# Three more weight slots for the experts, taken from tiles that the mixing has finished with

## What is computed

```python
for l in range(DEPTH):                                    # DEPTH = 2
    xn = rms_norm(x, norm_mix[l])
    c_q, c_kv, k_rope, dq, dk, dv, mu, mv, mo, mg = jnp.split(xn @ w_in[l], split_at, axis=-1)
    y_mla = mla_mixer(c_q, c_kv, k_rope, ...)
    y_dil = dilated_mixer(dq, dk, dv, rel_bias, ...)      # scores + a bias that depends on the distance
    y_ml = mlstm_mixer(mu, mv, mo, mg, ...)
    x = x + jnp.concatenate([y_mla, y_dil, y_ml], axis=-1) @ w_out[l]
    x = x + hier_moe(rms_norm(x, norm_ffn[l]), ...)

def hier_moe(x, wg, bg, we, be, w_gate, w_up, w_down):
    ...                                                   # comb: two experts for each token
    h = jax.nn.silu(jnp.einsum('bsd,edf->bsef', x, w_gate)) * jnp.einsum('bsd,edf->bsef', x, w_up)
    h = h * comb[..., None].astype(h.dtype)
    return jnp.einsum('bsef,efd->bsd', h, w_down)
```

## Time and profile before

| | us |
|---|---|
| median of 3 runs | 2033.39 |
| lowest and highest of them | 2032.96, 2038.36 |
| the profiled execution | 2034.52 |
| its span, first to last instruction | 2032.8 |
| PE busy in the span | 1945.6 |
| DVE busy | 472.4 |
| ACT busy | 318.0 |
| mean granted TensorE clock, share of full speed | 0.983 |

### The profile page before, as it was taken

The page is one execution under the profiler, slowest core; times in us unless marked ns, Lnnn a source line. Parts: engine busy times, 40 slices in busy tenths (PEclk is TensorE's granted clock), DMA queues, the critical chain, the costliest instruction groups (busy, mean ns, idle before and its releaser), DMA issues.

```text
span 2032.8 us, 26560 instructions
## 1 busy us (share of the span) xinstructions
PE 1945.6 (96%) x11730; PEld 1468.8 (72%) x11730; DVE 472.4 (23%) x1233; ACT 318.0 (16%) x831; POOL 4.8 (0%) x11
## 2 busy tenths in 40 slices
PE   6999999999889999999899999999998899999998
PEld 6788888788756666556597888877877556665555
DVE  2323223222201110221133241323221121110212
ACT  2122122210211100111022221221111111100110
POOL 0000000000000000000000000000000000000000
PEclk9999999999999999999999999999998999999999
DMA  8343342224499999999953333331255999999996
GB/s 322 149 188 124 125 152 97 88 83 165 192 425 420 412 428 406 407 404 405 427 195 158 132 125 124 125 130 42 88 200 237 426 409 411 406 428 409 404 408 272
DMA packets 39302, 536.03 MB, mean 264 GB/s; under 512 B 4648, under 2 KB 4776, under 8 KB 6672
## 3 DMA queue, kind: packets, MB, share of 16 engines
q1 hardware_dynamic: 38160, 531.46, 64.2%
q0 software_dynamic: 768, 2.77, 0.4%
q10 hardware_dynamic: 256, 0.04, 0.0%
HBM read 532.13 MB, written 2.12 MB: 263 GB/s over the span
## 4 chain that ended last, share of the span: by engine, by line
PE 95%; issue 3%; DVE 1%; DMA 1%; ACT 0%; SPq 0%; DVEq 0%
PE ps L624 93%; PE ps L675 1%; DMA ring<-in_w_lat 1%; PE ps L968 0%; PE ps L691 0%; PE ps L683 0%; PE ps L889 0%; PE ps L1008 0%; ACT PR L1831 0%; SPq L550 0%; PE ps L762 0%; ACT L1844 0%; DVE v_mla L1547 0%; PE ps L802 0%; DVE PR L1589 0%
## 5 line engine op out<-in xcount | busy, mean ns | idle before, releaser
L624 PE MATMUL ps<-ring,scr 128*64 128x256 f32 (+2 forms) x5184 | 717.2, 434 | 47.7 <-issue 47.0
L624 PEld LDWEIGHTS ps<-ring,scr 128*64 128x64 f32 (+1 forms) x5184 | 413.6, 141 | 339.1 <-issue 208.0
L624 PE MATMUL ps<-ring,XN 128*128 128x256 f32 (+2 forms) x2304 | 485.8, 372 | 16.6 <-DMA ring<-in_w_lat 16.6
L624 PEld LDWEIGHTS ps<-ring,XN 128*128 128x128 f32 x2304 | 425.7, 191 | 66.3 <-issue 18.5
L624 PE MATMUL ps<-XN,ring 128*128 128x256 f32 x768 | 170.4, 381 | 0.9 <-DVE prob L1137 0.9
L624 PEld LDWEIGHTS ps<-XN,ring 128*128 128x128 f32 x768 | 144.7, 190 | 26.6 <-issue 7.7
L624 PE MATMUL ps<-PR,ring 128*128 128x256 f32 x640 | 141.3, 380 | 0.0
L624 PEld LDWEIGHTS ps<-PR,ring 128*128 128x128 f32 x640 | 120.7, 190 | 18.6 <-issue 2.7
L624 PE MATMUL ps<-v_mla,PR 128*128 128x128 f32 x1024 | 121.7, 282 | 4.0 <-DVE v_mla L1547 4.0
L624 PE MATMUL ps<-prob,PR 128*128 128x256 f32 x512 | 120.0, 389 | 4.9 <-issue 3.9
L624 PEld LDWEIGHTS ps<-v_mla,PR 128*128 128x128 f32 x1024 | 120.2, 198 | 4.1 <-issue 4.1
(11 more groups left out here) (226 smaller groups left out, 907.2 us busy)
## 6 DMA issues: line engine op xcount, KB each, us to landing
ring<-in_moe_w_gate SPq DMA_DIRECT2D x64, 2048.0 KB, 12.8
ring<-in_moe_w_up SPq DMA_DIRECT2D x64, 2048.0 KB, 13.5
ring<-in_moe_w_down SPq DMA_DIRECT2D x64, 2048.0 KB, 17.6
ring<-in_w_main SPq DMA_DIRECT2D x36, 2048.0 KB, 8.0
ring<-in_w_out_a SPq DMA_DIRECT2D x10, 2048.0 KB, 7.9
ring<-in_w_out_b SPq DMA_DIRECT2D x6, 2048.0 KB, 8.1
ring<-in_w_lat SPq DMA_DIRECT2D x4, 1472.0 KB, 16.3
ring<-in_w_up SPq DMA_DIRECT2D x2, 1664.0 KB, 16.8
```

The costliest lines, as they stand in the source:

```text
L624: return pe.matmul(o, lhsT, rhs, start=start, stop=stop, skip_group_check=True)
```

## The change

It gives the expert half nine slots. The three new ones are no new memory: slot 6 (`IN_XN`) is the tile `XN`, slot 7 (`IN_PR`) is columns 5120 to 9215 of `PR`, slot 8 (`IN_BIAS`) is the first 4096 columns of `BIAS`. The expert loads go round in the order 8, 5, 0, 1, 2, 3, 4, 6, 7. The mixing half keeps its six, begun one place earlier (`c0` in slot 5). The first load into slot 8 may go once the last bias read, `ds11`, is done, those into 6 and 7 once `ob7` is. `Y` moves from `PR` to `prob`, `Sw` from `prob` to `PR`; `combB` and `comb2` move within `PR`. The bias is overwritten, so between the layers POOL reads it back from HBM once, after the last product that reads slot 8 in layer 0 (`u1` of the last pair), and DVE waits for that in layer 1.

```diff
+IN_XN, IN_PR, IN_BIAS = NSLOT, NSLOT + 1, NSLOT + 2
+EXPERT_SLOTS = (IN_BIAS, 5, 0, 1, 2, 3, 4, IN_XN, IN_PR)
...
 def plan_slots():
 
-    r = Uses(NSLOT)
+    r = Uses(NSLOT + 3)
     r.part = "layer"
-    at, held = 0, None
+    at, held = NSLOT - 1, None
...
     for j, name in enumerate(EXPERT):
-        r.once(name, j % NSLOT)
+        r.once(name, EXPERT_SLOTS[j % len(EXPERT_SLOTS)])
...
-        Sw = probf[0:2 * CAP, 0:S]
+        Sw = prf[0:2 * CAP, at + 704:at + 704 + S]
...
-        Y = prf[0:2 * CAP, 8192:8192 + D]
+        Y = probf[0:2 * CAP, 0:D]
...
+        spare = {IN_XN: xnf, IN_PR: prf[:, at + 1024:at + 1024 + SLOT],
+                 IN_BIAS: BIAS[:, :, :].rearrange("p h n -> p (h n)")[:, 0:SLOT]}
...
         def slot(name):
-            return ring[:, SLOTS.where(name), :]
+            s = SLOTS.where(name)
+            return ring[:, s, :] if s < NSLOT else spare[s]
...
             if at > 0:
                 return ready(LAST_READER.get(before, before), l)
+            if SLOTS.where(name) == IN_BIAS:
+                return copied(f"ds{H_D - 1}", l)
+            if SLOTS.where(name) in (IN_XN, IN_PR):
+                return ready(f"ob{N_OUT - 1}", l)
             return ready(LAST_READER[before], l - 1) if l else None
...
             pool.wait_ge(bias_out, 32)
+            for l in range(DEPTH - 1):
+
+                last = [n for n in EXPERT if SLOTS.where(n) == IN_BIAS][-1]
+                pool.wait_ge(*ready(LAST_READER[last], l))
+                pool.dma_start(BIAS[:, :, :], bass.AP(bias_dram.tensor, 0, [[1, P], [2 * S, H_D], [1, S + P]])).then_inc(bias_out, 16)
+                pool.wait_ge(bias_out, 48 + 16 * l)
...
-                                dve.wait_ge(bias_out, 32)
+                                dve.wait_ge(bias_out, 32 + 16 * l)
```

More of the change, by code:

```diff
@@ L393, in build @@
         iota = prf[:, at + 640:at + 640 + CAP]
-        combB = prf[:, at:at + NE * S].rearrange("p (e s) -> p e s", e=NE)
-        Y = prf[0:2 * CAP, 8192:8192 + D]
-        comb2 = prf[:, 10240:10240 + NT * NE].rearrange("p (t e) -> p t e", t=NT)
+        combB = prf[:, at + 1024:at + 1024 + NE * S].rearrange("p (e s) -> p e s", e=NE)
+        Y = probf[0:2 * CAP, 0:D]
+        comb2 = prf[:, at + 960:at + 960 + NT * NE].rearrange("p (t e) -> p t e", t=NT)
         q_mla, k_mla = PR[:, :, MV:MV + W_M], PR[:, :, MO:MO + W_M]
@@ L454, in grow @@
             return probf[0:H_M, at:at + S]
-        slot_full = [sem(f"slot_full{s}") for s in range(NSLOT)]
+        slot_full = [sem(f"slot_full{s}") for s in range(NSLOT + 3)]
         psum_full = [sem(f"psum_full{b}") for b in range(8)]
```

## The result

The changed kernel takes 1985.14 us (median of 4 runs, 1982.98 to 1986.55), the kernel before beside it 2034.16: a ratio of 0.9755, with a 95% interval of 0.9737 to 0.9772. That is 49 us less, where 56 had been forecast (1978). The profiled execution's span is 1984.9 us, against 2032.8: 47.9 less, and this is the difference that the rest of the text accounts for.

The account below looks back on a forecast made before the run. The prediction took the DMAs to bound the expert stages, just above TensorE. Gain 58.1 us, less 1.7 (clock) and 0.3 (reload), is 56.1: 2034.5 becomes 1978.4, median about 1978; own range 1973 to 1988, 8 in 10 1967 to 1993.

Parts of the forecast that it names:

- the reload hurts: Rival: the bias reload delays layer 0's last two expert loads, with upper bounds for reload and clock; 1986 us, chance 0.12.
- What bounds the kernel: Expert stages: DMAs bind at a full queue, 58.9 us a pair against TensorE's 57.1; TensorE ready 4 us before them.
- The floor of TensorE: Rival for the expert stages: TensorE is the bound, all waits and slow clock go, 66.2 us gained; 1968, chance 0.13.
- The rate of a full queue: Expert stages: about 427 GB/s from g0 of pair 0 to the last load, no dip where dn0 is read.
- the rivals at 413 and 358 GB/s: Expert loads: 413 GB/s whatever the queue, about 2004 us, chance 0.09; 358 through the new tiles, about 2135, chance 0.02.
- The tightest place, pair 0: After g1 of pair 0 nothing is freed for 15 us; 2.9 us of queue against 2 of start just holds.
- 83 loads and 3.8 us: From g0 of pair 0 to u1 of pair 7: 83 loads of 4.91 us plus 3.8 fixed; 58.1 us gained in all.
- The stretch: From SP's first issue after g0 of pair 0 to u1 of pair 7's start; the prediction's steps give 411.4 us.
- The clock behind the last waits: Last u1 of each layer: a slow clock costs up to 1.7 us each, 0 to 3.4; 1.7 taken.
- The reload: Bias reload beside layer 0's last expert loads: delays them 2.2 us, of which 0.3 shows; bounds 0 to 6.2.
- The mixing: Mixing half of the layers: counted as unchanged, with no term in the sum.
- two waits in pairs 6 and 7: Expert stage: PE's waits fall from 9 or 10 to about two, some 1.7 us before g1 and 2.3 before u1.

Follow-up runs that it names:

- half the bytes: Changed kernel, but from pair 1 on each expert load brings only its first half: 1964.48 us, ratio 0.9657.
- 128-row copy: Changed kernel plus one ACT copy of 0.26 MB within SBUF in pair 1 of each expert stage, as 128 rows: 1983.98 us.
- 127-row copy: Changed kernel plus one ACT copy of 0.26 MB within SBUF in pair 1 of each expert stage, as 127 rows: 1997.24 us.
- without the prefetch: Changed kernel with nine slots, but the seventh expert load and all behind it wait until g0 of pair 0 is done: 2012.26 us.
- fewer instructions on PE: Changed kernel with every second product step of the experts left out, all loads kept: 1965.19 us, ratio 0.9655.

## Why the prediction was right, and what was off

**The time and the rivals.** 1985 lies in the forecast's own range, 1973 to 1988, but it is nearer to the rival *the reload hurts* (1986) than to 1978. The time alone could not have told them apart. The run without the reload does, against the rival: the 7 us are elsewhere, as the account below shows.

**What bounds the kernel.** Right. The floor of TensorE is 1964.5 measured, 1968 by the prediction's steps; the DMAs stand above it at 1985. TensorE would have been ready 10 us before the DMAs, not 4: the DMAs came 2.5 us late, the stage began 1.0 us later, and TensorE's own work from there to u1 of pair 7 is 405.3 us (half the bytes), where I had 407.3.

**The rate of a full queue.** Right: 427 GB/s in both stages, no dip where dn0 is read. That new tiles fill more slowly (the rivals at 413 and 358 GB/s) is refuted by the same two windows; also the Trainium skill's 358 GB/s (DMA: Bandwidth & Descriptors, Where 436 GB/s comes from) doesn't hold for one core streaming alone here.

**The tightest place, pair 0.** It just held, as worked out: 405 GB/s at 575 to 580 and no wait for loads behind it.

**83 loads and 3.8 us.** The step that was off. The stretch was 413.9 and 414.1 instead of 411.4: 2.5 and 2.7 us too little. The fixed part came from a queue that had just drained, where the engines are together; at the end of 83 loads eight of them are 4.5 to 5.4 us behind the first. Each load alone costs a bit less (4.90), the last wait a good deal more. The landings and the experiments show the cause and its size: three fetches on each of eight engines at 1.5 us are 4.5 us of lag; nine fetches fewer, 1.7 us less; a lag made by hand, 7.5 us more. The prediction's step had no term for what single engines have to do beside the stream.

**The clock behind the last waits.** I took one slow u1 of two. Both were slow: dn of pair 7 begins 16.29 us after u1 in either layer (975.69 and 1958.66 above), before 14.6. That is 1.7 us more in each, 3.4 in all, the upper of my bounds. It isn't fixed by the kernel: with the 128-row copy the same distance was 16.1 us in layer 0 and 14.6 in layer 1, with seven slots, with the 127-row copy and without the prefetch 14.6 in layer 0, all behind waits of 2.26 to 2.50 us. So one of two was a fair guess, and this execution had two; the changed kernel run again had two as well.

**The reload.** I took 0.3 of 0 to 6.2; it was nothing on the path. The delay of the last load, 1.9 us, came out close to the 2.2 worked out from the packets. But without the reload that load would have come 21.0 us after u1, where I had 19.6, and only the slow clock at u1, which put dn1 off by 1.7 us, gave back the time. So that term came out at nothing by luck.

**The mixing.** I counted it unchanged. It was longer by 1.0 us in layer 0 (SP's first release after g0 came at 545.54 for 544.58) and by 2.0 in layer 1. No wait is new there. The clock was longer at half. In layer 0 it falls in both kernels around the pause of 3.9 us ahead of the router's products and stays at half for 6.8 us before and 10.2 in the changed kernel. A window over that place, the kernel before and then the changed one:

```profile
522.50:533.00 10.50, 7.51 (x46) 7.47 (x47) 3.71 (x22) 1.73 (x6) 0.00 (x0) 0.67 0.23 100
```

```profile
522.50:533.00 10.50, 8.01 (x37) 7.96 (x38) 3.04 (x19) 1.14 (x4) 0.00 (x0) 0.51 1.00 429
```

In layer 1 the clock of the changed kernel fell once more, for some 3 us in a stretch full of products and with no DMA at work at all:

```profile
1379.00:1384.00 5.00, 5.00 (x16) 4.11 (x17) 1.78 (x6) 1.92 (x8) 0.00 (x0) 0.66 0.00 0
```

The products that this second fall hits have a row on the page of the changed kernel (first below) and on that of the kernel without the reload (second):

```profile
L642 PE MATMUL ps<-PR,ring 128*128 128x256 f32 x640 | 142.9, 383 | 0.0
```

```profile
L636 PE MATMUL ps<-PR,ring 128*128 128x256 f32 x640 | 141.3, 380 | 0.0
```

The changed kernel run again shows the slower value, and so do the kernels with seven slots and with fewer instructions on PE. The one with the 128-row copy, whose edit lies elsewhere, and the other seven, the kernel before among them, show the faster. So it seems to belong to an execution and not to the change. One or two traces of a kernel don't prove that, and what sets it off I don't know.

**The account.** 56.1 forecast, less 5.15 (u1 late in both layers), less 1.7 (second slow u1), plus 0.3 (reload), less 2.95 (mixing), plus 1.2 (the last scatter of layer 0 took 8.83 us, in the trace of before 10.06) makes 47.8, against 47.9 measured. PE's busy time fell by 16 us though its work is the same: before, 21.3 us of it were slow clock behind the waits ahead of g1, and most of these waits are gone.

Against the forecast, "two waits in pairs 6 and 7" turned out as four in pairs 5 to 7, up to 2.65 us long: with the engines apart and TensorE some 2 us quicker than reckoned, the lead over it is used up one pair earlier. That is argued from the figures above; no run separates the two.

## What to carry to other kernels

When a ring of slots feeds TensorE near the DMAs' full rate, find first the step that drains the queue: here one slot more all but ended it and was worth 29 of the 49 us, the load that it prefetches among them; the next two are worth only what they prefetch. Count a queue that never drains to the landing of its slowest engine: keep single-engine transfers (such as the 127 rows here) and long instruction streams on other engines out of such a stage, and don't trust the mean rate, which hides both. Ask of every tile that is idle in the stage whether it can hold a load, even if its content must be fetched again. But count what that costs the loads beside it: here 1.9 us on the last load, hidden by a slow product ahead of it in one kernel, and a wait of 2.25 us in another.

## What was unexpected of the hardware

- The sixteen DMA engines drift apart in a stream without a gap: 1.3 us at load 10, 5.4 at load 92. Drained about once in a pair, they stay within 0.7 to 2.5 us.
- TensorE's instruction fetches (16 KB packets, 23 in 402 us) fall on eight of the engines, and each puts its engine some 1.5 us behind, though its packet takes 1.06. POOL's (8 KB) fall on one, 0.65 us each; 26 more of them cost 14 us, though they are 0.13% of the bytes.
- Granted clock and waits: a g1 behind a wait of 1.98 us took 8.81 us, one behind 1.63 took 7.13, and before one behind 2.65 took 7.13 too. Waits of 2.26 to 2.50 us ahead of the last u1 had either sequel. So the length of the wait alone doesn't decide. With no waits at all (half the bytes) the window's clock stood at 1.00.
- In a stretch of products without a pause the clock still fell to half for some 3 us, in 4 of the 12 profiled executions.
